# A Trainium2 kernel: the first mixer's projections, gate and output as three products of rounded parts

## What is computed

```
def mix(h, s0f, s0b):                       # gdn_mixer, first mixer
    q, k, v, z, g, beta = project(h)        # p = h @ w_in; q, k, v: conv over tokens, silu; q, k: l2norm
    of, sf = gated_delta_scan(q, k, v, g[:, :, 0], beta[:, :, 0], s0f)
    ob, sb = gated_delta_scan(_rev(q), _rev(k), _rev(v), _rev(g[:, :, 1]), _rev(beta[:, :, 1]), s0b)
    o = (of + _rev(ob)).astype(h.dtype)
    o = rms_norm(o, norm_g) * jax.nn.silu(z)
    return o.reshape(b, t, GDN_VW) @ w_out, sf, sb
```

## Time and profile before

| | us |
|---|---|
| three runs | 4130.40, 4116.75, 4127.23 |
| median | 4127.23 |
| span of the profiled execution | 4131.5 |
| TensorE busy | 3788.0 (92%) |
| VectorE busy | 1836.7 (44%) |
| ScalarE busy | 942.2 (23%) |
| GpSimd busy | 354.9 (9%) |
| matmuls of the first mixer's projections (L1238), both pieces | 253.9 |

### The profile page before, as it was taken

How to read it: one execution, slowest core, us unless ns; L and a number is a source line. 1 busy time by engine, 2 the same in 40 slices (tenths; PEclk the granted TensorE clock), 3 DMA queues, 4 the chain that set the end, 5 groups by cost and what they waited for, 6 DMA issues and landing times.

```text
span 4131.5 us, 50603 instructions
## 1 busy us (share of the span) xinstructions
PE 3788.0 (92%) x21228; PEld 2328.2 (56%) x21228; DVE 1836.7 (44%) x2915; ACT 942.2 (23%) x1862; POOL 354.9 (9%) x929
## 2 busy tenths in 40 slices
PE   7989999998999998999988988888698998998999
PEld 4578656865534443777766762222255433446777
DVE  3656456654012221588885530111326467415443
ACT  3421133123111011456564121000115100100000
POOL 0033002301000000000000000000040157000000
PEclk8989999998999999799999989999898999999999
DMA  5241131312598896212111429999721112231331
GB/s 199 84 127 47 51 132 56 119 63 83 224 384 337 337 369 245 100 57 82 52 41 41 133 93 381 421 421 421 270 78 41 34 50 57 75 102 51 102 102 51
DMA packets 278564, 631.29 MB, mean 153 GB/s; under 512 B 63553, under 2 KB 205377, under 8 KB 219457
## 3 DMA queue, kind: packets, MB, share of 16 engines
q1 hardware_dynamic: 275712, 627.40, 41.2%
q10 hardware_dynamic: 2624, 0.66, 0.1%
HBM read 611.75 MB, written 16.25 MB: 152 GB/s over the span
## 4 chain that ended last, share of the span: by engine, by line
PE 67%; DMA 11%; DVE 10%; ACT 3%; POOL 3%; SPq 3%; issue 3%; ACTq 0%; DVEq 0%
PE ps L1894 11%; PE ps L1595 11%; PE ps L1238 6%; PE ps L1945 5%; PE ps L1601 4%; DMA arena<-moe_w_down 4%; DMA arena<-moe_w_gate 2%; PE ps L1502 2%; PE ps L2118 2%; PE ps L1480 2%; PE ps L1753 2%; PE ps L1748 2%; PE ps L1744 2%; DMA arena<-moe_w_up 2%; DVE arena L3488 2%
## 5 line engine op out<-in xcount | busy, mean ns | idle before, releaser
L1595 PE MATMUL ps<-arena 128*64 128x512 f32 x3072 | 709.4, 601 | 79.3 <-DMA arena<-moe_w_down 23.0
L1595 PEld LDWEIGHTS ps<-arena 128*64 128x64 f32 x3072 | 207.4, 137 | 529.4 <-issue 385.2
L3225 DVE SCALAR_TENSOR_TENSOR arena<-arena,ps 128x512 f32<-128x512 f32 (+1 forms) x48 | 30.2, 656 | 525.1 <-PE ps L1595 525.1
L1238 PE MATMUL ps<-arena 128*128 128x512 f32 (+1 forms) x768 | 253.9, 489 | 3.5 <-DVE g_rows L2882 2.1
L1945 PE MATMUL ps<-arena 128*128 128x512 f32 x512 | 229.6, 605 | 5.0 <-DVE arena L3488 4.3
L3488 DVE TENSOR_TENSOR arena<-arena,ps 128x512 f32<-128x512 f32 x86 | 58.4, 687 | 372.4 <-ACT arena L2769 143.6
L1748 PE MATMUL ps<-h_first,w_rest 128*128 128x512 f32 (+1 forms) x576 | 208.9, 379 | 0.6 <-DVE arena L3384 0.5
L1238 PEld LDWEIGHTS ps<-arena 128*128 128x128 f32 x768 | 145.9, 191 | 105.8 <-issue 93.6
L3233 DVE TENSOR_TENSOR m_yx_rest<-ps,m_yx_lead 64x512 fp32r<-64x512 f32 x64 | 44.1, 689 | 363.0 <-ACT m_yc_lead L2484 205.6
L1744 PE MATMUL ps<-h_second,w_rest 128*128 128x512 f32 (+1 forms) x576 | 196.1, 355 | 0.4 <-DVE h_second L3291 0.4
L2484 ACT ACTIVATE m_yx_lead<-ps 64x512 fp32r<-64x512 f32 x64 | 37.8, 591 | 662.3 <-PE ps L1595 661.5
(11 more groups left out here) (496 smaller groups left out, 6990.6 us busy)
## 6 DMA issues: line engine op xcount, KB each, us to landing
arena<-moe_w_gate SPq DMA_DIRECT2D x128, 1024.0 KB, 9.3
arena<-moe_w_up SPq DMA_DIRECT2D x128, 1024.0 KB, 10.7
arena<-moe_w_down SPq DMA_DIRECT2D x128, 1024.0 KB, 11.8
arena<-ada_w SPq DMA_DIRECT2D x48, 1024.0 KB, 5.0
arena<-ffn_w_gate_up SPq DMA_DIRECT2D x22, 1024.0 KB, 5.0
arena<-gdn_w_in SPq DMA_DIRECT2D x16, 1024.0 KB, 8.9
arena<-w_in SPq DMA_DIRECT2D x30, 512.0 KB, 3.8
arena<-ssd_w_x SPq DMA_DIRECT2D x8, 1024.0 KB, 4.8
```

Source lines behind the costliest of these rows:

```text
L1238: mm = pe.matmul(ps[:, 2 * (i % 2) + j, 0:nn], state.w[:, k, m * P:(m + 1) * P], hT[:, k, c0:c0 + nn], start=(k == 0), stop=(k == KD - 1))
L1595: mm = pe.matmul(ps[CAPX * h:CAPX * h + CAPX, bank, :], x[:, 0:CAPX], w[:, 512 * h:512 * h + 512], **flags)
```

## The change

- **Products.** `split_product` is moved ahead of the first mixer and takes the lead tiles of h as an argument. The projections (`gin`), the gate (`gz`) and the output (`gout`) use it or its pattern: three products of fp32r parts in place of one fp32 product.
- **Parts of the weights.** ScalarE makes each chunk's lead (`chunk_lead`). The rest is VectorE's (`chunk_rest`) for the projections but for the first chunk of a half; that one and those of `gz` and `gout` are GpSimd's (`POOL_RESTS`), ahead of its inverses and behind them.
- **Parts of h and o.** VectorE casts h to `g_hi` and, when the tail has used `hT`, writes the rest into `hT`'s place. o's leads come from ScalarE (`leads`), its rests from VectorE (`rests`); the output waits for them head by head.
- **Ring.** While the first mixer runs, raw chunks and `ada` chunks use the slots 0 to 2, leads the slots 3 and 4 (or, for two of the gap's chunks, raw), and slot 5 holds `g_hi` for k = 6, 7. Three gap chunks, not one, are now issued inside `low_blocks`.
- **Tail.** `gdn_tail` puts token tile t into the 32-row group t mod 4: 48 products of 128 columns in place of 16 of 512 and 256; it is copied and turned accordingly.
- Several semaphores of the router are merged into `route_mm`, `level_masks` is dropped, and the two `ada` rows move; no work changes with these. The slots behind the first mixer shift.

```
@@ slots() @@
+    oldest = lambda places: min(places, key=lambda x: last[x])
     for item in PLAN:
-        if item[0] in EXPERTS:
+        if item in GDN_ITEMS:
+            a = oldest(GDN_RAW + GDN_LEAD if item in GAPS else GDN_RAW)
+        elif item[0] in EXPERTS:
...
-        if item in PARTED:
-            b, parted = NARROW + parted % (RING - NARROW), parted + 1
+        if item in PARTED and item[0] != "gout":
+            if item in GDN_ITEMS:
+                b = oldest(GDN_LEAD)
+            else:
+                b, parted = NARROW + parted % (RING - NARROW), parted + 1
             lead[item] = (b, last[b])
...
@@ GpSimd @@
-            for n in range(2 * PAIRS):
-                low_inverse(n)
+            for hg in range(GH // HG):
+                chunk_rest(FIRST_GIN[hg])
+                for n in range(hg * PAIRS, (hg + 1) * PAIRS):
+                    low_inverse(n)
+                for kind in ("gz", "gout"):
+                    for n in range(2):
+                        chunk_rest((kind, hg, n))
@@ TensorE @@
-                    for bank, (c0, nn, _) in ((2, XSET), (3, CSET)):
-                        mm = pe.matmul(ps[0:4 * GH, bank, 0:nn], w[:, k, :], hT[:, k, c0:c0 + nn], start=(k == 0), stop=(k == KD - 1))
+                    for t in range(NT):
+                        r, c = tail_at(t)
+                        mm = pe.matmul(ps[r, 2 + t // 4, 0:P], w[:, k, :], hT[:, k, t * P:(t + 1) * P], start=(k == 0), stop=(k == KD - 1))
...
+            def split_product(out, item, w, cols_, x, high, tail_from=None):
+                wh, wl = w
+                rests = lambda k: pe.matmul(out, wh[:, k, cols_], hT_lo[k][:, x], start=False, stop=(tail_from is not None and k == KD - 1))
+                for k in range(KD):
+                    if tail_from:
+                        pe.wait_ge(s.h_lead, tail_from[0](k))
+                    pe.matmul(out, wh[:, k, cols_], high[k][:, x], start=(k == 0), stop=False)
+                    if not tail_from:
+                        rests(k)
+                pe.wait_ge(*rest_of_chunk(item))
+                for k in range(KD):
+                    mm = pe.matmul(out, wl[:, k, cols_], high[k][:, x], start=False, stop=(tail_from is None and k == KD - 1))
+                for k in range(KD if tail_from else 0):
+                    pe.wait_ge(s.h_rest, tail_from[1](k))
+                    mm = rests(k)
+                return mm
...
                     if i % 2 == 0:
-                        state.w = take(("gin", PARTS[i // 4], hg, (i // 2) % 2))
+                        state.w = split_chunk(item)
...
-                        for k in range(KD):
-                            mm = pe.matmul(ps[:, 2 * (i % 2) + j, 0:nn], state.w[:, k, m * P:(m + 1) * P],
-                                           hT[:, k, c0:c0 + nn], start=(k == 0), stop=(k == KD - 1))
+                        mm = split_product(ps[:, 2 * (i % 2) + j, 0:nn], item, state.w, slice(m * P, (m + 1) * P), slice(c0, c0 + nn), g_hi,
+                                           (lambda k: k + 1, lambda k: k + 1) if hg == i == j == 0 else None)
...
-                w = [take(("gout", hg, 0)), None]
-                w[1] = take(("gout", hg, 1))
-                pe.wait_ge(s.go_o, HG * (hg + 1))
+                w = [split_chunk(("gout", hg, 0)), None]
+                for n in range(2):
+                    pe.wait_ge(*rest_of_chunk(("gout", hg, n)))
+                w[1] = split_chunk(("gout", hg, 1))
...
+                            if m == b == 0:
+                                pe.wait_ge(s.go_rest, HG * hg + j + 1)
+                            wh, wl = w[j // 2]
+                            for n, (left, right) in enumerate(((wh, o_hi), (wh, o_lo), (wl, o_hi))):
+                                mm = pe.matmul(ps[:, b + 2 * (m % 2), 0:nn], left[:, j % 2, m * P:(m + 1) * P], right[j][:, c0:c0 + nn],
+                                               start=(j == 0 and n == 0), stop=(j == HG - 1 and n == 2))
@@ ScalarE @@
                             if k:
                                 ada_row(3)
+                                chunk_lead(FIRST_GIN[0])
...
                         for u in range(2):
                             decays(0, u)
+                    if i % 2 == 0 and i < 10:
+                        chunk_lead(("gin", PARTS[(i + 2) // 4], hg, (i // 2 + 1) % 2))
...
+                    if p in (3, 4):
+                        chunk_lead(("gz", hg, p - 3))
...
                 gates(0)
+                chunk_lead(("gout", hg, 0))
                 gates(1)
                 roots(2)
                 roots(3)
+                leads(0)
+                leads(1)
                 gates(2)
+                chunk_lead(("gout", hg, 1))
+                leads(2)
                 gates(3)
+                leads(3)
+                if hg + 1 < GH // HG:
+                    chunk_lead(FIRST_GIN[hg + 1])
@@ VectorE @@
+            for k in range(KD):
+                dve.wait_ge(s.h_ready, 2 * k + 2)
+                v.do(dve.tensor_copy(g_hi[k][:, :], hT[:, k, :]), s.h_lead)
+            dve.wait_ge(s.w_used, USED[("gtail",)])
+            v.settle()
+            for k in range(KD):
+                v.do(dve.tensor_tensor(hT_lo[k][:, :], hT[:, k, :], g_hi[k][:, :].bitcast(F32), ALU.subtract), s.h_rest)
...
+                    if i % 2 == 0 and i < 10:
+                        chunk_rest(("gin", PARTS[(i + 2) // 4], hg, (i // 2 + 1) % 2))
...
                     v.do(dve.tensor_tensor(oT[:, j, :], oT[:, j, :], pre[j % 2][:, 0:N], ALU.mult), s.go_o)
+                    if j:
+                        rests(j - 1)
+                rests(HG - 1)
```

More of the change, by code:

```diff
@@ L154 @@
 USED = {item: n + 1 for n, item in enumerate(PLAN)}
-PARTED = [x for x in PLAN if x[0] in ("sx", "sbc", "sz")]
-THIN = PARTED + [("stail",)] + sum((ADA[b] for b in ADA_SSD.values()), [])
+PARTED = [x for x in PLAN if x[0] in ("gin", "gz", "gout", "sx", "sbc", "sz")]
+THIN = [x for x in PARTED if x[0][0] == "s"] + [("stail",)] + sum((ADA[b] for b in ADA_SSD.values()), [])
+GAPS = sum((sum(ADA[b:b + 3], []) for b in ADA_GAP), [])
+GDN_ITEMS = PLAN[PLAN.index(("gtail",)):PLAN.index(("gout", GH // HG - 1, 1)) + 1]
 EXPERTS = ("eg", "eu", "ed")
@@ L185 @@
 SPLITS = PARTED
+FIRST_GIN = [("gin", PARTS[0], hg, 0) for hg in range(GH // HG)]
+POOL_RESTS = [x for x in SPLITS if x in FIRST_GIN or x[0] in ("gz", "gout")]
+VEC_RESTS = [x for x in SPLITS if x not in POOL_RESTS]
 class Lane:
@@ L210, in __init__ @@
         self.mask_done = new("mask_done")
-        self.level_masks = new("level_masks")
         self.vec_steps = new("vec_steps")
@@ L279, in __init__ @@
         self.resid = new("resid")
-        self.lg_mm = new("lg_mm")
+        self.route_mm = new("route_mm")
         self.sm_sub = new("sm_sub")
@@ L396, in rounded_tiles, with plain_tile @@
                 return [scope.enter_context(nc.sbuf_tensor(f"{name}{i}", [P, size], F32R)) for i in range(count)]
+        def plain_tile(name, start, size):
+            with ExitStack() as scope:
+                scope.enter_context(nc.sbuf_tensor("before_" + name, [P, start], F32))
+                return scope.enter_context(nc.sbuf_tensor(name, [P, size], F32))[:, :]
         def whole_tiles(name, count, size):
@@ L1473, in gates @@
                     i = hg * HG + j
+                    item = ("gz", hg, j // 2)
                     if j % 2 == 0:
[L1475 removed]
+                        state.w = split_chunk(item)
                     if i >= 2:
@@ L1478, in gates @@
                     for b, (c0, nn, _) in enumerate((XSET, CSET)):
-                        for k in range(KD):
-                            mm = pe.matmul(ps[:, 2 + b + 2 * (j % 2), 0:nn], state.w[:, k, (j % 2) * P:(j % 2) * P + P],
-                                           hT[:, k, c0:c0 + nn], start=(k == 0), stop=(k == KD - 1))
+                        mm = split_product(ps[:, 2 + b + 2 * (j % 2), 0:nn], item, state.w, slice((j % 2) * P, (j % 2) * P + P), slice(c0, c0 + nn), g_hi)
                     mm.then_inc(s.w_used if j % 2 else s.go_z, 1)
@@ L1739, in ssd_scalars @@
                 mm.then_inc(s.tl_spread, 1)
-            def split_product(out, item, w, cols_, x, tail_last=False):
-                wh, wl = w
-                rests = lambda k: pe.matmul(out, wh[:, k, cols_], hT_lo[k][:, x], start=False, stop=(tail_last and k == KD - 1))
-                for k in range(KD):
-                    if tail_last:
-                        pe.wait_ge(s.h_lead, 2 * k + 2)
-                    pe.matmul(out, wh[:, k, cols_], hT_hi[k][:, x], start=(k == 0), stop=False)
-                    if not tail_last:
-                        rests(k)
-                pe.wait_ge(s.w_rest, SPLITS.index(item) + 1)
-                for k in range(KD):
-                    mm = pe.matmul(out, wl[:, k, cols_], hT_hi[k][:, x], start=False, stop=(not tail_last and k == KD - 1))
-                for k in range(KD if tail_last else 0):
```

(6 more changed lines are left out.)

109 lines of the change are left out of this document (65 added, 44 removed).

## The result

The changed kernel takes 4106.73 us (median of six runs, 4103.04 to 4114.71) against 4129.57 before (six runs, 4116.75 to 4132.97). The ratio is 0.9947, 95% interval 0.9932 to 0.9961: faster by 22.8 us where 47 were forecast. The direction and the range (4053 to 4107) held, the last by a hair. The size did not.

What follows compares the result with a forecast made beforehand. TensorE, busy for 92% of the span, was taken as the bound where it is waited for. Stage gains summed to 46.9 us, giving span 4084.6; with the profiled span 4.3 above the runs' median, the forecast was 4080, range 4053 to 4107.

Steps and rivals of the forecast that it cites:

- Price of a tile: Projection tile on TensorE as products of rounded parts: 8.30 us against 10.32, a gain of 2.0 each.
- The second half's way to T3: Start of the second half to the end of its tile 3: 42.8 us before, 34.5 after, gain 8.3.
- The new wait: Behind tiles 3 and 7 of each half a chunk is requested late: landing 6.9 us, next tile 9.0 after.
- The clock: TensorE may run at its lower level after each idle gap: 2.0 us charged per gap, ends 0 and 3.5.
- B: End of tile 3 to end of tile 7, each half: 49.4 us before, 49.0 after, gain 0.4.
- C: End of tile 7 to the first matrix written out, each half: 50.0 us before, 50.5 after, -0.5.
- Rivals 1 and 4: Loads land in 5.3 and clock holds, 4064 us, chance 0.18; lower clock lasts a whole tile, 4112, chance 0.08.
- A: Kernel start to the end of the first half's tile 3: 105.0 us before, 94.4 after, gain 10.6.
- E: Gates and output, each half: 90.3 us before, 75.2 after, gain 15.1, with 1.1 charged for contention with GpSimd.
- D: The recurrence itself, each half: change of 0, bounds 0 and -4 us.
- G: Behind the first mixer: second mixer's tail chunk earlier, +1.5 us; its first output chunk later, -3.5.
- Rival 3: Chunks land late behind tiles 3 and 7, both halves: slower, 4149 us at a landing of 24.1; chance 0.06.

## Why the prediction was right in its direction and wrong in its size

**Price of a tile: right.** Without stalls four tiles, their sums and the small products take 41.6 us. That is 4 x 8.30 + 8.4 where before it was 4 x 10.32 + 8.1. The second half's way to T3, +7.8, is four tiles at 2.0 less 0.3.

**The new wait: right in place, high by 1.2.** Landing 5.8 instead of 6.9, four times. The clock fell at every gap, as charged: 1.7 instead of 2.0. This made B and C better than forecast by 3.8 in all. Rivals 1 and 4 are out: the clock neither held nor stayed low for a tile.

**A: the casts of h were not in the sum.** I took the lead tiles of h as made when ScalarE had h ready. The change has VectorE cast them, eight times, behind h; and GpSimd's rest of chunk one, at the same moment, was in no sum either. Held by it, two casts lost 3.6 us. Part of that was hidden: h was ready at 47.7, earlier than the 49.0 of the sum, and the rests of h started at 50.7 instead of 49.7. The lower clock behind them (57.8 to 62.5, 1.3 us) was not in the sum either. Measured 8.4 for 10.6.

**E: contention was mis-sized, and the output's overlap misread.** I took 1.1 a half from a row of additions and put 4.4 into the high end. It was 4.4: a rest of o, with both operands in SBUF, ended only behind GpSimd's instruction. (GpSimd's rows in both traces name SBUF tiles alone, never `ps`; that it works on PSUM, as said at the start, is not so here.) I had the reasoning that reciprocals are most of the chain right, and missed that the one instruction that starts beside GpSimd's pays the whole of it. Further I let the output run three heads ahead; the code orders the third head's rest behind the last gate product, so it was two, and TensorE stopped and came back at the lower clock (456.7 to 463.5 in this execution). Of the 5.3 missing in the first half 3.3 are contention beyond the 1.1, and 2.0 the output. Measured 9.8 and 10.8 for 15.1.

**D: the recurrence is not 0 in one execution.** 219.8 and 224.7 against 222.9 and 217.3. In the ten experiments it took 215.3 to 221.3 in the first half and 215.0 to 219.5 in the second, without a pattern by kernel: the 224.7 is the largest of all. So some 5 of the missing 28 are this execution's own. It is also the slowest of its six, 8 us above their median, which fits with the medians differing by 22.8 and the spans by 18.6. What makes it scatter (each pair of steps crosses DRAM three times) was not looked into. A loss of 4 a half by the late ada loads is not to be seen: the ten experiments average 218.6 a half, the two halves before the change 220.1.

**G: the step that failed.** "Downstream" had two terms, and both were right: the output chunk's, and the tail's (TensorE's wait for it fell from 2.81 to 1.29). What the new order of the ring does to the four `ada` chunks was put at nothing. Before, two of them left in the middle of the gates and output (901.24, 924), and at the end of the first mixer one expert chunk was on its way when the router's load was issued. The new ring makes all four wait for the last output chunk, and eight loads of 1 MB share the DMA engines with the router's. I looked at what stands behind each moved load on its own queue and who waits for its landing, and not at a small load of another queue at that time. From the last residual to the router's product it was 23.2 us instead of 12.0, 11.2 of waiting, and the product's 32 records took 12.38 instead of 10.32, at a granted clock of 0.85 instead of 1.00: 13.3 together. Rival 3, "chunks land late, up to 24.1", named the right mechanism at the wrong place: the ring's own loads landed in 5.6 to 5.8.

The sum of the 28.3: A 2.2, E 9.6, D 4.3, the second half's way 0.5, less 3.8 in B and C, makes 12.8; behind the first mixer 13.3 for the router, 3.4 - 3.5 = 0 for the output chunk, and 2.1 that lie in the experts and the second mixer. Those 2.1 are within the 11 us over which this part scatters, and their cause is open. The changed kernel's diff also sets the size of the program's DMA scratch space, which the description of the change leaves out; no experiment separates it, and all experiments share it.

## What to carry to other kernels

When a ring's slots are reassigned, list the moments at which several loads become free to go at once, and every load of any queue that is issued then: a small one in small packets pays for all the large ones. Give GpSimd elementwise work only where VectorE has reciprocals, work with an operand in PSUM, or nothing; a subtraction that is cheap on VectorE can cost it more on GpSimd. When an edit adds a stream of leads and rests, put every cast and every order of two lines into the sum: the exchange of two ScalarE lines was worth 4 us a half.

## What the runs showed of the hardware

- A load of 64-byte packets beside loads of 8 KB packets on another queue took 4.3, 6.7 (8.2 in another kernel) and 23.1 us with 8, 16 and 64 large packets an engine between its issue and its landing; in front of them, on the same queue, 2.3.
- VectorE's instructions with two SBUF operands, and its fp32 cast to fp32r with one, wait for the end of a GpSimd subtraction that runs beside them (5.37 for 0.96, 2.37 for 1.02, two casts 4.66 for 1.02). A reciprocal of 128x768 does not: 4.94 to 4.97 with and without. Nor does an addition with one operand in PSUM: the pair of residuals at 465.15 took 1.14 beside GpSimd's subtraction of 462.47 to 467.08, and 1.14 without. GpSimd's own 2048-column subtraction took 4.55 to 4.89.
- After 4.3 to 4.4 us of idleness TensorE's granted clock was at its lower level for 3.4 us at each of the four gaps, and at 1.00 in the whole stretch when the gap was taken away.
